# Paged attention: which queue issues the K and V pages (SP, GpSimd and ACT instead of SP and GpSimd)

## The reference

```python
def diff_attn_paged(q, k, v, lam, k_pool, v_pool, page_table):
    kp = k_pool[page_table].reshape(bsz, -1, H_B, 2, DB).astype(F32)
    vp = v_pool[page_table].reshape(bsz, -1, H_B, 2 * DB).astype(F32)
    s_past = jnp.einsum('bqhmd,bkhmd->bhmqk', qf, kp)
    s_new = jnp.einsum('bqhmd,bkhmd->bhmqk', qf, k.astype(F32))      # causal among the 4 new tokens
    s = jnp.concatenate([s_past, s_new], axis=-1) * (DB ** -0.5)
    wts = diff_weights(s, lam)                                       # softmax(map 0) - lam * softmax(map 1)
    return (jnp.einsum('bhqk,bkhe->bqhe', wts[..., :past], vp)
            + jnp.einsum('bhqk,bkhe->bqhe', wts[..., past:], v.astype(F32)))
```

## Time and profile before

| | us |
|---|---|
| median of 3 runs | 6399.69 (6394.83 to 6410.55) |
| the profiled execution's own time | 6396.28 |
| its span | 6394.6 |
| first K page issued in the stage | 1378.69 |
| first apply, and POOL's next V page | 1483.71, 1486.86 |
| last K page issued | 1954.9 |
| last V page issued | 2054.29 |
| DMA of `oT` issued | 2063.30 |

### The profile page before, as it was taken

One profiled execution on the slowest core, in us unless ns is written; L12 is line 12 of the kernel. 1 busy time (PEld: TensorE's weight loads), 2 busy tenths in 40 slices (PEclk: granted clock), 3 DMA queues, 4 the chain that ended last, 5 costly groups with the idle time before them and its releaser, 6 DMA issues. The chain is left out here.

```text
span 6394.6 us, 91697 instructions
## 1 busy us (share of the span) xinstructions
PE 5373.8 (84%) x35012; PEld 3320.6 (52%) x35012; DVE 2374.2 (37%) x5477; ACT 1506.7 (24%) x3428; POOL 852.0 (13%) x1191
## 2 busy tenths in 40 slices
PE   6988999976553574667899999999899999998898
PEld 4644455543332464246655565555655565565554
DVE  1146655522221444501434334433534343432322
ACT  2235443311110211001212122212212222211211
POOL 0012211113443111001100011001101011000000
PEclk9999999987776676567899999999899999999999
DMA  2111111136774100033122222223122312223232
GB/s 84 47 30 34 33 34 35 33 92 194 230 227 127 41 14 22 11 117 100 40 76 82 84 65 77 75 82 103 47 74 84 91 54 77 76 74 92 69 92 76
DMA packets 719749, 494.62 MB, mean 77 GB/s; under 512 B 78474, under 2 KB 688522, under 8 KB 719279
## 3 DMA queue, kind: packets, MB, share of 16 engines
q1 hardware_dynamic: 680337, 400.31, 21.5%
q0 software_dynamic: 24576, 67.14, 3.6%
q10 hardware_dynamic: 14400, 21.31, 0.9%
HBM read 439.44 MB, written 49.19 MB: 76 GB/s over the span
## 5 line engine op out<-in xcount | busy, mean ns | idle before, releaser
L3492 PE MATMUL s_f_b<-s_f_h,s_f_W 128*128 128x416 f32 x4480 | 1636.8, 521 | 25.8 <-DMA s_f_h<-o_t 16.9
L3492 PEld LDWEIGHTS s_f_b<-s_f_h,s_f_W 128*128 128x128 f32 x4480 | 844.0, 192 | 700.7 <-issue 683.2
L3550 PE MATMUL s_f_b<-s_f_a,s_f_W 128*128 128x416 f32 x1760 | 634.1, 516 | 0.2
L532 PE MATMUL s_p_acc<-s_hT,s_p_W 128*128 128x416 f32 x1600 | 620.3, 534 | 9.1 <-DMA s_p_W<-in_w_in_dram 9.1
L3550 PEld LDWEIGHTS s_f_b<-s_f_a,s_f_W 128*128 128x128 f32 x1760 | 328.4, 190 | 263.5 <-issue 257.4
L532 PEld LDWEIGHTS s_p_acc<-s_hT,s_p_W 128*128 128x128 f32 x1600 | 297.1, 194 | 284.3 <-issue 265.1
L1327 POOL DMA_DIRECT2D s_V<-in_cache_diff_v_dram x512 | 274.8, 537 | 401.3 <-issue 399.5
L3751 DVE TENSOR_TENSOR s_f_xT<-s_f_xT,s_f_b 128x416 f32<-128x416 f32 x160 | 93.5, 586 | 587.1 <-PE s_f_b L3550 533.3
L3772 POOL TENSOR_TENSOR s_f_ex<-s_f_ex,s_f_mix 128x416 f32<-128x416 f32 x105 | 111.7, 1064 | 1306.2 <-ACT s_f_mix L3578 1305.6
L1097 ACT ACTIVATE s_prob<-s_s_ps,s_ntop 128x512 f32<-128x512 f32 (+3 forms) x320 | 196.4, 619 | 367.9 <-DVE s_ntop L1148 367.9
L1351 PE MATMUL s_tp<-s_ident,s_K 128*128 128x128 f32 x1024 | 167.7, 319 | 115.7 <-DMA s_K<-in_cache_diff_k_dram 113.2
(11 more groups left out here) (688 smaller groups left out, 8204.4 us busy)
## 6 DMA issues: line engine op xcount, KB each, us to landing
s_f_W<-in_ffn_w_in_dram SPq DMA_DIRECT2D x220, 512.0 KB, 3.8
s_K<-in_cache_diff_k_dram SPq DMA_DIRECT2D x512, 128.0 KB, 2.9
s_V<-in_cache_diff_v_dram POOLq DMA_DIRECT2D x512, 128.0 KB, 2.9
s_f_W<-in_ffn_w_out_dram SPq DMA_DIRECT2D x80, 448.0 KB, 3.6
cols_t<-s_p_out ACTq DMA_DIRECT2D x100, 208.0 KB, 1.9
s_f_W<-in_w_out_dram SPq DMA_DIRECT2D x40, 512.0 KB, 4.2
s_f_W<-in_ffn_w_out_dram SPq DMA_DIRECT2D x40, 512.0 KB, 3.9
s_r_c<-cols_t SPq DMA_DIRECT2D x16, 704.0 KB, 6.5
```

What stands on the lines that cost most here:

```text
L532: mm = pe.matmul(self.acc[n % 2][:, 0:CH], self.W[:, u, k, :], self.hT[:, k, c * CH:(c + 1) * CH], start=(k == 0), stop=(k == KD - 1))
L3492: mm = pe.matmul(bank(u)[:, 0:G], w[:, k, :], h[:, k, :], start=(k == 0), stop=(k == KD - 1 and kind != "op"))
L3550: mm = pe.matmul(bank(u)[:, 0:G], w[:, k, :], a[:, f % NA, :], start=(k == 0), stop=(k == len(part) - 1))
```

## The change

Of every group's four K pages and four V pages the fourth is issued by ACT, each on a semaphore of its own (`k_act`, `v_act`). SP issues the other three K pages, POOL the other three V pages, and PE waits for both semaphores of a group. On ACT the first eight K pages are issued ahead of its first copy. From step 1 on a K page (of the group seven steps ahead) follows the `turn` of each step. V pages follow the K page, at most one to a step: `v_slot` places them at the first step whose transposes stand behind the apply that frees the slot, so in the steady part the V page of group g stands in step g + 14.

```diff
--- before.py
+++ after.py
@@ -1269,6 +1269,12 @@
         init, zeroed, padded = st.sem("init"), st.sem("zeroed"), st.sem("padded")
         k_in = [st.sem(f"k_in{j}") for j in range(KG)]
         v_in = [pr.whole.sem(f"v_in{j}") for j in range(VG)]
+        k_act, v_act = [st.sem(f"k_act{j}") for j in range(KG)], [st.sem(f"v_act{j}") for j in range(VG)]
+        applied = lambda a: 16 * (a // 4 + 1) + (5, 8, 11, 14)[a % 4]
+        v_slot, at = {}, 1
+        for g in range(G):
+            at = max(at + 1, applied((g - VG) // 4) + 1 if g >= VG else 0)
+            v_slot.setdefault(at, []).append(g)
         flipped, kt_act, kt_dve, scored, copied, topped, exped = (
             st.sem(x) for x in ("flipped", "kt_act", "kt_dve", "scored", "copied", "topped", "exped"))
         crossed, drained, lowered, repeated, factored, weighed, inverted, scaled, combed, pv, held = (
@@ -1305,7 +1311,7 @@
                 for g in range(G):
                     if g >= KG:
                         sp.wait_ge(flipped, place[("k", g - KG, 1)] + 1)
-                    for i in range(4):
+                    for i in range(3):
                         page = sp.value_load(table[0:1, g * 4 + i:g * 4 + i + 1], min_val=0, max_val=n_pool - 1)
                         sp.dma_start(K[:, g % KG, i, :], kp[bass.ds(page, 1)].rearrange("a p h d -> p (a h d)"))\
                           .then_inc(k_in[g % KG], 16)
@@ -1344,7 +1350,8 @@
                         pe.wait_ge(drained, cross[job] - 1)
 
                 def flip_k(g):
-                    pe.wait_ge(k_in[g % KG], 64 * (g // KG + 1))
+                    pe.wait_ge(k_in[g % KG], 48 * (g // KG + 1))
+                    pe.wait_ge(k_act[g % KG], 16 * (g // KG + 1))
                     for h in range(2):
                         dst = bank(("k", g, h))
                         for i in range(4):
@@ -1402,7 +1409,8 @@
                         turned(("t", b, 4))
                     for j in range(4):
                         g = 16 * b + 4 * s + j
-                        pe.wait_ge(v_in[g % VG], 64 * (g // VG + 1))
+                        pe.wait_ge(v_in[g % VG], 48 * (g // VG + 1))
+                        pe.wait_ge(v_act[g % VG], 16 * (g // VG + 1))
                     for i in range(4):
                         for j in range(4):
                             g = 16 * b + 4 * s + j
@@ -1454,6 +1462,21 @@
             def _(act):
                 act.preload_act_table_set("natural_log_exp_and_others")
 
+                def page_of(g):
+                    return act.value_load(table[0:1, g * 4 + 3:g * 4 + 4], min_val=0, max_val=n_pool - 1)
+
+                def k_page(g):
+                    if g >= KG:
+                        act.wait_ge(flipped, place[("k", g - KG, 1)] + 1)
+                    act.dma_start(K[:, g % KG, 3, :], kp[bass.ds(page_of(g), 1)].rearrange("a p h d -> p (a h d)"))\
+                       .then_inc(k_act[g % KG], 16)
+
+                def v_page(g):
+                    if g >= VG:
+                        act.wait_ge(pv, (g - VG) // 4 + 1)
+                    act.dma_start(V_[:, g % VG, 3, :], vp[bass.ds(page_of(g), 1)].rearrange("a p h d -> p (a h d)"))\
+                       .then_inc(v_act[g % VG], 16)
+
                 def turn(job):
                     act.wait_ge(flipped, place[job] + 1)
                     src = tp[place[job] % NT]
@@ -1482,10 +1505,17 @@
                     act.wait_ge(drained, cross[("mB", b)])
                     act.activation(fac[:, :], top[:, :], ACT.Exp, scale=scale, bias=nm[:, :]).then_inc(factored, 1)
 
+                act.wait_ge(init, 16)
+                for g in range(KG):
+                    k_page(g)
                 for b in range(NB + 1):
                     for k in range(16):
                         if b < NB:
                             turn(("k", 16 * b + k, 0))
+                        if 1 <= 16 * b + k <= G - KG:
+                            k_page(16 * b + k + KG - 1)
+                        for g in v_slot.get(16 * b + k, []):
+                            v_page(g)
                         if b and k == 3:
                             exps(b - 1)
                         for x in plan.get(k, "").split() if b else []:
```

## The result

The changed kernel takes 6237.22 us, the median of 3 runs (6233.00 to 6243.49), against 6399.69: a ratio of 0.9744 (95% interval 0.9720 to 0.9768), faster by 162.5 us. The forecast was 6254 us in a range of 6222 to 6325.

The account below looks back on a forecast made before the run. Page issue on two queues was taken as the paged stage's bound. From the profiled 6396.3 us, -167.0 (lead -24.8, main part -142.2) + 14 + 7 gave 6250.3, or 6254 us against the median, range 6222 to 6325.

Parts of the forecast that it names:

- The bound was the issue of the queues: Paged stage: SP and POOL issue 512 pages each, at 1.128 and 1.185 us a page, and set its pace.
- "it doesn't do what it says" rival: Paged stage: memory sets the pace and the queues only follow, so no change, 6400 us; chance 0.03.
- The lead, -24.8: Stage start to first apply: SP issues 66 K pages instead of 88, saving 24.8 us.
- POOL's main part, -142.2 before friction: After the first apply POOL issues 360 V pages instead of 480, saving 142.2 us; windows and DMA engines counted separately.
- ACT's page, 1.12 us, beside its computing: ACT's queue: a page read and issue costs 1.12 us, two a step 2.23, overlapping its computing.
- The windows, 14 us: Seven steps from p3 to next p0: ACT's pages stretch 21.4 us to 25.5, POOL waits; 2 us in each of 7.
- DMA engines, 7 us: While K and V overlap, 302 GB/s asked for just fills the engines; 2% of 359 us, 7 us lost.
- The sum: Whole kernel: -167.0 + 14 + 7 on the profiled 6396.3 us gives 6250.3; 6254 against the median.
- the end: From the last V issue to the stage's last DMA: stays at 9.0 us.
- The rivals with a dear page on ACT: ACT's queue: 2.0 us a page makes it the bound, 6320 us, chance 0.13; from 2.15 us slower than before, chance 0.05.
- the ceiling at 251 GB/s: Rival, paged stage: DMA engines cap at about 251 GB/s, costing 45 us instead of 7, 6292 us; chance 0.12.

Follow-up runs that it names:

- Both halves: From the changed kernel, ACT issues only the fourth K pages (6371.81 us), or only the fourth V pages (6341.83 us); the other queue keeps all four.
- The second group's order: Changed kernel with ACT's two pages of a step behind that step's exponentials and t copies: 6234.58 us, against 6242.03 for the changed kernel beside it.

## Why the prediction was right, and where its sizes were off

- **The bound was the issue of the queues.** Right. Both halves, the whole and the constant page numbers agree. The two queues could have moved more: with the pages' addresses known they move 340 GB/s instead of 228, so the "it doesn't do what it says" rival is out (6400 forecast, 6237 measured). The sentence of the Trainium skill (DMA: Bandwidth & Descriptors, section Issuing engines are not separate DMA queues) that the issue is "usually small relative to the DMA itself" does not hold here: 1.13 us of issue against 131,072 bytes at 349 GB/s, 0.38 us. (A single page needs 2.9 us from issue to landing, more than its issue; but several are under way at once, and then a queue's pace is what counts.) That the queues share the same engines, its other half, does show: the landing time rises with every queue's rate (2.9, 3.8, 6.9 us).
- **The lead, -24.8.** Measured -26.4, and the run with K pages alone shows it by itself.
- **POOL's main part, -142.2 before friction.** Measured 431.9 us against 426.6: friction 5.3 us.
- **ACT's page, 1.12 us, beside its computing.** 1.06 us, beside it. With twice as many pages ACT is the bound, at this price.
- **The windows, 14 us.** The mechanism was right: exponentials later, p0 later, POOL behind it. The size was not: four waits, 6.7 us, in place of seven of 2 us, so this term was 7.3 us too dear. The last window has no K step behind it and takes 16.4 us; two others are covered by a pause of 2.9 us that POOL's queue makes anyway. And they came to 23.0 to 25.0 us, not 25.5. The forecast had 1.9 us from the pages behind five copies (2.0 measured, 16.8 against 14.8) and 2.2 us from two pages in front of the copy of t0: these passed beside the exponentials and cost nothing. The second group's order gives those 7 us back.
- **DMA engines, 7 us.** This step failed. A share that several queues are billed for is no measure of how full the engines are; the ceiling is 349 GB/s and the demand 302. What room is left for it in the main part: 360 pages at POOL's neighbour distance of 1.15 us are 414.0, its three own pauses 6.8 above the usual gap, the four waits 6.7; that leaves 4.4 us of 431.9. The same count before the change (552.0, five pauses 10.8) leaves 4.6 of 567.4 for 480 pages. So a microsecond or two at most. The fuller engines show in the landing times.
- **The sum.** -26.4 - 135.5 + 0.6 = -161.3 us in the stage, where -146.0 was forecast. The 15.3 us between them are 1.6 in the lead and 14.3 in the main part, less 0.6 at the end; the 14.3 are in the main the 7 us too many for the windows and the 7 for the DMA engines, both too pessimistic. The 17 us between 6254 and 6237 are these 15.3 and the 3.4 by which the profiled execution before was under its median, less 2.1 by which the stages around this one are longer in the profiled execution after.
- **The rivals with a dear page on ACT** (2.0 us as the bound, 2.15 us and more as slower) are out by the rows of ACT's issues, 1.06 us, and the ceiling at 251 GB/s by 294 GB/s in the main part.

What the prediction did not look at is the 0.79 us beside SP's DMA: it was taken as a fixed price to be shared among three engines. 0.27 us of it is a table read, which four pages can share for 0.30.

## What to carry to other kernels

Where a queue issues at an even pace and waits for nobody, split the pace into its instructions before adding a queue: here reading four numbers at once brings 138 us on two queues, and, with the comparison of bounds left out, 245 us, more than a third queue's 162. A page that a compute engine's queue issues comes as late as that engine's own work lets it: place it by when its reader needs it, with the landing time at full rate. A ceiling of the DMA engines is a rate seen over many slices with rising landing times, not a share divided into a rate. A queue that also feeds a compute pipe can take DMAs at their bare price, but count how many stand between its computing and whoever waits for that.

## What the runs showed of the hardware

- A read of a table in SBUF into registers: one number 269 ns on SP, 290 on POOL, 282 on ACT; four numbers 297 and 328; three numbers 667 and 729.
- 128 KB pages on two queues stand at 345 to 352 GB/s in 28 of 40 slices (constant page numbers, 340 on average; 344 with the table's pages and light reads), with queue shares that add up to 1.04, landing after 5.8 to 6.9 us.
- Register reads, arithmetic and DMA issues of ACT's queue pass beside a running ACTIVATE (pages issued at 1690.94 and 1692.00 under exponentials that end at 1692.15).
- POOL's queue pauses for 2.8 us every 88 pages before the change and for 2.9 every 93 after it; nothing that the profile shows is waited for.
- A third issuing queue can cost time where two already fill the engines, 6181.65 us against 6151.53; it did so when it issued both K and V pages, and not with either alone (6140.49 and 6143.80).
- After a wait of 7.3 us the same 32 matmuls took 3.64 us at a granted clock of 0.50, against 1.93 us at 1.00.
